# C's value loads of the next unit but one, moved ahead of C's key loads of the unit behind it, in ScalarE's program

## What is computed

```
A: oa = dilated_attend(qa, cache_a ++ ka, cache_a ++ va)      # 6 heads, cache contiguous
B: ob = dsa_attend(qb, top-k of an indexer, cache_b pages)    # 6 heads, pages by page_table
C: oc = diff_attend(qc, kc_all, vc_all)                       # 4 heads, pages by page_table
   kc_all = concat([paged_rows(cache_c_k), kc])
   vc_all = concat([paged_rows(cache_c_v), vc])
   a = p[:, :, 0] - lam_full * p[:, :, 1];  o = a @ v_all;  RMS-normed per head
x = layer_norm(ALPHA * x + (1 + g) * (concat(oa, ob, oc) @ w_o))
x = layer_norm(ALPHA * x + (1 + g) * (square(relu(h @ w_up)) @ w_down))
```

## Time and profile before

| | |
|---|---|
| median of the three runs | 1344.26 us |
| the profiled execution | 1343.05 us |
| its span, first to last instruction | 1341.3 us |
| TensorE busy | 1278.7 us (95%) |
| VectorE, ScalarE, GpSimd busy | 495.3, 265.1, 59.6 us |
| mean granted TensorE clock | 0.99 |
| DMA moved | 363.83 MB, mean 271 GB/s |

### The profile page before, as it was taken

The page is one execution under the profiler, slowest core; times in us unless marked ns, Lnnn a source line. Parts: engine busy times, 40 slices in busy tenths (PEclk is TensorE's granted clock), DMA queues, the critical chain, the costliest instruction groups (busy, mean ns, idle before and its releaser), DMA issues.

```text
span 1341.3 us, 23207 instructions
## 1 busy us (share of the span) xinstructions
PE 1278.7 (95%) x8038; PEld 802.4 (60%) x8038; DVE 495.3 (37%) x1433; ACT 265.1 (20%) x683; POOL 59.6 (4%) x265
## 2 busy tenths in 40 slices
PE   6899999989899999999999999999999999999998
PEld 2444356645557666666666545664556577767775
DVE  1203568766482111011040165876666411101113
ACT  0111144422223010000022212542221401100001
POOL 1000011100000000000010000110000100000000
PEclk9999999989999999999999999998999999999999
DMA  9899999999873777968754687999996366676663
GB/s 376 248 324 288 294 331 342 348 346 352 295 234 140 240 277 251 337 232 328 275 213 157 225 286 277 359 339 351 354 353 233 141 219 219 225 259 219 216 210 138
DMA packets 190814, 363.83 MB, mean 271 GB/s; under 512 B 23072, under 2 KB 141608, under 8 KB 189034
## 3 DMA queue, kind: packets, MB, share of 16 engines
q1 hardware_dynamic: 156192, 345.62, 74.7%
q10 hardware_dynamic: 34506, 16.74, 4.7%
HBM read 354.20 MB, written 58.40 MB: 308 GB/s over the span
## 4 chain that ended last, share of the span: by engine, by line
PE 63%; SPq 22%; issue 5%; DMA 5%; DVE 3%; DVEq 1%; ACT 1%; ACTq 0%
PE psf L1148 23%; PE psf L1623 21%; SPq L556 18%; PE psf L1526 4%; DMA ring<-in_tiles 4%; PE psf L1607 3%; PE psf L1169 2%; PE psf L1465 2%; SPq L566 2%; SPq L548 2%; PE psf L1232 1%; PE psf L1521 1%; PE psf L1261 1%; PE psf L1350 1%; PE psf L1179 1%
## 5 line engine op out<-in xcount | busy, mean ns | idle before, releaser
L1148 PE MATMUL psf<-hT,ring 128*128 128x320 f32 x1184 | 324.6, 434 | 4.9 <-DMA ring<-in_tiles 4.7
L1148 PEld LDWEIGHTS psf<-hT,ring 128*128 128x128 f32 x1184 | 223.1, 190 | 108.5 <-issue 14.1
L1623 PE MATMUL psf<-big,ring 128*128 128x320 f32 x1024 | 278.0, 433 | 2.1 <-DVE big L2113 2.1
L1623 PEld LDWEIGHTS psf<-big,ring 128*128 128x128 f32 x1024 | 193.7, 190 | 86.8 <-issue 3.4
L2113 DVE TENSOR_TENSOR big<-sq 128x320 f32<-128x320 f32 x64 | 31.5, 492 | 239.2 <-ACT sq L1117 238.9
L1723 DVE TENSOR_SCALAR rstd<-psf,adaT 128x256 f32<-128x256 f32 x40 | 19.3, 482 | 235.6 <-PE psf L1623 232.0
L1117 ACT ACTIVATE sq<-psf 128x320 f32<-128x320 f32 x64 | 28.0, 437 | 231.9 <-PE psf L1148 220.9
L1350 PE MATMUL psf<-big,qs 128*32 128x512 f32 x512 | 67.5, 622 | 5.9 <-DMA big<-in_pool_bk 5.5
L1074 ACT ACTIVATE sq<-xT 128x320 f32<-128x320 f32 x32 | 15.0, 470 | 289.8 <-DVE xT L1736 276.6
L1397 PE MATMUL psf<-big,ptbuf 128*32 128x128 f32 x2048 | 66.3, 283 | 6.3 <-DMA big<-in_pool_cv 6.0
L1397 PEld LDWEIGHTS psf<-big,ptbuf 128*32 128x32 f32 x2048 | 57.0, 114 | 13.7 <-issue 11.7
(11 more groups left out here) (219 smaller groups left out, 1346.8 us busy)
## 6 DMA issues: line engine op xcount, KB each, us to landing
ring<-in_tiles SPq DMA_DIRECT2D x246, 512.0 KB, 4.5
big<-in_cache_a SPq DMA_DIRECT2D x64, 768.0 KB, 7.4
out_cache_a<-in_cache_a SPq DMA_DIRECT2D x64, 768.0 KB, 5.6
big<-in_pool_bk SPq DMA_DIRECT2D x128, 192.0 KB, 6.1
big<-in_pool_bv SPq DMA_DIRECT2D x128, 192.0 KB, 7.1
big<-in_pool_cv SPq DMA_DIRECT2D x192, 64.0 KB, 5.4
big<-in_tiles SPq DMA_DIRECT2D x22, 512.0 KB, 7.6
big<-in_pool_ck SPq DMA_DIRECT2D x128, 64.0 KB, 4.3
```

The costliest lines, as they stand in the source:

```text
L1148: ins = pe.matmul(ps[:, 0:T], ring[:, s, k, :], rhs[:, k, :], start=k == 0, stop=k == KD - 1)
L1623: ins = pe.matmul(bank[6 + m % 2][:, 0:T], ring[:, s, k, :], uT[:, KD * q + k, :], start=q + k == 0, stop=q == 3 and k == KD - 1)
```

## The change

The block that reads the page numbers and loads C's keys of unit n+3 goes from ahead of the late feature's copy and of C's values of unit n+2 to behind both. Nothing is added or removed: the same 64 key DMAs and 32 value DMAs per layer are issued by ACT, at other places of its program. `was` is set before either block, as it was, and so the values still use the page numbers that were read a unit ago.

```
                     was = at
-                    if NB <= u.n + 3 < UNITS:
-
-                        at = pages(UNIT[u.n + 3].b, CHECKED)
-                        load_c_keys(UNIT[u.n + 3], at)
                     if u.n in PLACED_BY_ACT:
                         ...
                     if u.n + 1 < len(LATE):
                         feature(LATE[u.n + 1], late_bank(u.n + 1))
                     if NB <= u.n + 2 < UNITS:
                         act.wait_ge(u_o.sem, u_o.done(l, u.n))
                         load_c_values(UNIT[u.n + 2], was)
+                    if NB <= u.n + 3 < UNITS:
+
+                        at = pages(UNIT[u.n + 3].b, CHECKED)
+                        load_c_keys(UNIT[u.n + 3], at)
                     for k in slots[1:]:
                         exp_item(k)
```

## The result

| | before | after |
|---|---|---|
| median of 4 runs, us | 1345.74 (1342.4 to 1351.33) | 1364.07 (1363.7 to 1366.11) |
| ratio to before, 95% interval | 1 | 1.0151 (1.0129 to 1.0174) |
| profiled span, us | 1341.3 | 1364.3 |
| DMA waits of TensorE on C's keys | none | 9.1 us, 4 times |
| TensorE waiting for ACT's copy (L990) | none | 13.7 us, 4 times |

The change costs 18.3 us by these medians (1.4%) and 1.5% by the ratio. The ratios of this document are estimates over all runs beside each other and not quotients of the medians, so that the two differ by up to 0.15%. Two slow runs, one at 1493.63 us of the kernel with unit 6 alone and one at 2613.52 us of the kernel before on the same chip, are left out of the ratios. I had forecast 1346 us in a range of 1341 to 1356, so both the number and the range missed it. The two last rows of the table are from the profiled executions.

A forecast was written before the change was run, and what follows sets the result against it. The prediction took the full DMA engines fetching SP's pages as the bound, TensorE close behind. Stalls mostly taken up by page waits left +1 us in layer 0 and +2 in layer 1: 1343.05 + 1 + 2 = 1346 us, range 1341 to 1356.

The forecast's parts named there:

- The stalls in units 5 and 6: TensorE waits in the logits' last part for ACT's delayed turned_unit: 2.8 and 3.4 us, 6.2 us per layer.
- The lowered clock: Low clock behind page waits at units 9 and 10 no longer paid: 1.9 us in layer 0, 5.6 in layer 1.
- only earlier: Layer 1's clock falls in the changed kernel too, behind unit 6's new stalls; 2 to 5 us kept.
- SP's pause: Before issuing unit 10's keys, SP pauses 2.4 us in layer 0, 0.5 at most in layer 1, costed at nothing.
- DMA share below 1 around 270 us (SP starved): Sign of a wrong forecast, together with the output projection starting late by 6 us or more.
- What TensorE no longer waits for: Page waits and low clock around units 9 and 10 absorb lateness: 6.3 us in layer 0, 8.3 in layer 1.
- C's keys of units 10 and 15: Only these two units can find C's keys late, by 0 to 2 us each.
- C's keys as the new bound: Rival, chance 0.12: keys 2 to 3 us late at units 10 and 15 of both layers, about +8 us, 1351.
- The sum: Over the profiled execution's 1343.05 us, +1 in layer 0 and +2 in layer 1: 1346 us.
- Nothing is taken up: Rival, chance 0.20: stalls of 6.2 us per layer stay; 1355.5 us, or 1359.5 with 2 us low clock per layer.
- The second rival: The same as "C's keys as the new bound": chance 0.12, about +8 us, 1351.

The follow-up runs named there:

- unit 6 alone: The kernel before with the new order in unit 6 only, the old one elsewhere: 1347.37 us, ratio 1.0008 to before.
- the filler: Matmuls whose results nobody reads, ahead of the stalls in logits 7 and 8, added to the kernel with units 5 and 6 moved: 1353.71 us, ratio 1.0065.
- units 5 and 6 alone: The kernel before with the new order in units 5 and 6 only; units 7 to 12 keep the old one: 1356.13 us, ratio 1.0094.
- both edits: The kernel with units 5 and 6 moved, plus unread matmuls in the stalls and SP signalled after the logits' second part: 1348.78 us, ratio 1.0034.
- the last experiment: The kernel before with unread matmuls ahead of the waits of logits 10, values 9 and logits 15: 1342.45 us, ratio 0.9986.
- the early signal alone: The kernel with units 5 and 6 moved, SP told the key slot is free after the logits' second part, not the third: 1354.36 us, ratio 1.0081.
- unit 12 alone: The kernel before with the new order in unit 12 only, which loads C's keys of unit 15: 1349.26 us, ratio 1.003.
- unit 7 alone: The kernel before with the new order in unit 7 only, which loads C's keys of unit 10: 1343.84 us, ratio 0.9986.
- units 7 to 12 alone: The kernel before with the new order in units 7 to 12; units 5 and 6 keep the old one: 1351.92 us, ratio 1.0066.

## Why the prediction was wrong, by its steps

**The stalls in units 5 and 6: right.** Forecast 2.8 and 3.4 us; measured 2.83 and 3.62 us in layer 0, 2.83 and 4.45 us in layer 1, 13.7 against 12.4 us in all. The issue time of 4.4 and 3.9 us in front of the copy is what set it. The sentence cited from the Trainium skill (DMA: Bandwidth & Descriptors, "Issuing engines are not separate DMA queues"), that issuing usually costs little beside the DMA itself, agrees with the rows for one DMA: about 0.5 us to issue against 5.5 us from issue to landing. What does not follow from it is that the moved block costs nothing, for eight of them stand ahead of a copy of 0.27 us that TensorE waits for. Its other half, that all queues share the same engines, is tested by no run here.

**The lowered clock: the step that failed first.** I gave back the low clock of before (1.9 us in layer 0 and 5.6 in layer 1, with what it lengthens there), wrote that the clock would fall in the changed kernel too, "only earlier", and kept 2 us for it in layer 1 and none in layer 0. In fact the clock fell behind each of the four stalls. Steps 6 and 7 are 21.2 us longer for stalls of 13.7: 7.5 us go to slower matmuls, of which the two groups of values in layer 0 show 1.55 and 1.17 us. (That the rest is the clock's is worked out and not measured matmul by matmul.) With the filler the same steps are only 0.7 to 1.2 us longer than the fillers' own 16.1. By the same measure as in the last experiment, "only earlier" is true of units 5 and 6 alone: 10.2 us against 11.9 before (and 5.1 with the filler, 0.0 with both edits). In the whole change it is 20.4 us. There the lowered clock is added and not moved, for C's late keys brought it back at logits 10 (0.57 from 293 to 301 us) and 15 (0.54 from 355 to 362 us). The filler runs value the part behind the stalls at 4 to 6 us of the total, with what the filler saves of SP's pause in it.

**SP's pause: 7.1 us in layer 0 and 6.1 in layer 1, where I had put 2.4 and 0.5 at most and costed them at nothing.** I put unit 8's last logits 6.2 us later. They came at 276.25 against 264.13; less the 4.1 us by which this execution is later from the start, that is 8.0 us, since the clock adds to the stalls. SP had 3.5 us in hand before (the logits with their mask done at 264.5, the keys issued at 268.34, of which 0.3 us are the way from one to the other), and had itself come 1.6 us further ahead in this execution: 8.0 - 3.5 + 1.6 = 6.1 us of pause, on top of the 1.1 us between the same two issues before. "Its DMAs land 5 to 7 us after issue, so the engines have work meanwhile" is wrong for 7 us: the share fell to 0.46. The text had named this very sign ("DMA share below 1 around 270 us (SP starved)") as what would prove it wrong, together with a late start of the output projection, which came 13.7 us late (370.9 against 357.2 us). What the pause costs is not shown: the early signal alone left the sum of SP's gaps at 13.1 us, and 2 to 4 us is what the signal is worth by the ratios.

**What TensorE no longer waits for: right with units 5 and 6 alone, undone by unit 7.** I took up 6.3 us in layer 0 and 8.3 us in layer 1. With units 5 and 6 alone, the step of values 9 gives back 5.3 and 6.7 us, and with 0.8 us in step 8 of layer 1 that is 12.8 us of the 14.6 (11.2 by steps 8 to 11). In the whole change it is 1.2 and 5.0 us (6.2 by steps 8 to 11), since unit 10's C keys are late.

**C's keys of units 10 and 15: mis-sized.** Charged with 2 and 1.5 us (unit 10) and 1 and about 0.4 us (unit 15); measured waits 2.52 and 2.84 us, then 2.00 and 1.74 us in layer 1, each with the lowered clock behind it in layer 0. Two terms are at fault, and which one differs by place. At unit 10 it is the time at which TensorE asks. I took about 12 us from the end of values 7; before, it was 10.8 us in layer 0 (267.73 to 278.56) and in the changed kernel 10.8 us in both layers (281.47 to 292.29, 942.91 to 953.75). At unit 15 of layer 0 it is the landing. The last key DMA was issued at 349.17 and TensorE went on at 356.66, 7.5 us later, where I had used the median of 5.5 us and asked 6.5 us of the rival. At the other three places this time is 6.0, 5.0 and 5.8 us. With unit 12 alone it was 8.2 us in layer 0 (issued by 339.95, on at 348.15), and with unit 7 alone 7.5 us (issued by 277.13, on at 284.64). TensorE needs all eight DMAs, so the median is too short for the last of them. C's keys as the new bound had 0.12 with 1351 us; that rival by itself is the kernel with units 7 to 12 alone, and it gives 1351.92 us.

**The sum.** Over both layers the forecast was 12.4 (stalls) less 11.1 (given back at logits 10, net of late keys) plus 1.7 (behind it) = 3 us. Measured by the same division of the steps: 21.2 (steps 6 and 7), less 6.2 (steps 8 and 9), plus 4.7 (steps 10 to 15) = 19.7 us. The first term is 8.8 us off for the clock (7.5) and for the stalls (1.3), the second 4.9 us, in which C's late keys of unit 10 are, the third 3.0 us, in which those of unit 15 are with the clock behind them. SP's pause has no line of its own in this division: what it costs is spread over the steps.

**The rivals.** "Nothing is taken up", at 1359.5 us with its low clock, is nearest in time, but partly by luck. Its condition held in part: SP's keys of unit 10 left 4.4 us later in layer 0 and 3.5 us later in layer 1, counted from the end of values 5, while TensorE was 8.0 us late in layer 0. And something is taken up: with units 5 and 6 alone, steps 6 and 7 are 21.6 us longer and the stretches 9.9. The time is made of more than this rival said. The second rival was true at the same time, and the two are not independent of each other: late C keys use up the very slack that should absorb the stalls. I had given each a chance and the sum of both none. Hence the range, which ended at 1356, left out the case in which both come.

**Left open.** What SP's pause costs, since no run took it out; and how the 6.6 us at step 9 divide between the keys' lateness and the clock. The two halves measured apart (1.0094 and 1.0066) add up to 1.0160, and the whole is 1.0151: that they add is no sign that the halves are independent, as unit 12 alone and unit 7 alone (together 1.0016) show against 1.0066 for units 7 to 12. This last difference is not explained: the runs of that kernel lie between 1346.27 and 1357.82 us, and its profiled stretches are only 3.7 us longer.

## What to carry to other kernels

DMAs issued by a computing engine are instructions in its stream: before moving a block of them, look for the first small copy behind it and who waits for that, and charge the stall with the slower clock behind it. Then count the reserve once: if two edits both make use of the same wait (here 5.3 and 6.7 us at logits 10), the second pays in full, so a forecast needs the case in which all of them come together. For a load that needs all of its DMAs, take the longest landing seen in full queues and not the median (here 7.1 us before, and even that was passed by up to 1.1 us), and read the time at which the engine asks from the row of that very unit.

## What the hardware showed that I had not expected

- A TensorE stall of 2.8 to 4.5 us in work that is otherwise dense was followed each time by matmuls at the lower of the two clock levels: 64 value matmuls took 3.50 and 3.12 us instead of 1.95. Matmuls that nobody reads in the stall's place held the clock up, and by the ratios the kernel became 0.3 to 0.5% faster for work added (runs without overlap in the case of 0.5%).
- A queue that stops issuing for 7.1 us drains engines that had been at a share of 1.0: 0.46 and 0.53 over the two windows of 4 us from 272 to 280 us, although the page DMAs of this kernel have landing medians of 4.8 to 5.9 us on the page of the profile. In layer 1, after a gap of 6.1 us, the share was 0.57 for one such window.
- With the DMA engines full, TensorE went on 5.0 to 8.2 us after the last of eight 64 KB DMAs had been issued, in the whole change and in the kernels with unit 7, unit 12 and units 7 to 12 alone, where the median from issue to landing before was 5.5 us and the longest 7.1.
